# A decoder step with 32 experts: the last down rows in halves and narrowing blocks, the round count read earlier, the input scaled ahead of its squares' sum

## What is computed

```python
def _rmsnorm(x, g):
    xf = x.astype(jnp.float32)
    y = xf * lax.rsqrt(jnp.mean(xf * xf, axis=-1, keepdims=True) + NORM_EPS)
    return (y * g.astype(jnp.float32)).astype(x.dtype)
...
    def expert_block(args):
        xblk, e = args
        return (jax.nn.silu(xblk @ w_gate[e]) * (xblk @ w_up[e])) @ w_down[e]
...
    x = x + _hier_moe(_rmsnorm(x, norm_ffn_g), router_coarse, router_fine,
                      exp_w_gate, exp_w_up, exp_w_down)
```

## Time and profile before

| | |
|---|---|
| median of 3 runs | 1900.24 us (1899.46 to 1901.64) |
| the profiled execution | 1900.5 us |
| its span, first to last instruction | 1898.7 us |
| PE, DVE, ACT busy, share of the span | 82%, 33%, 14% |
| PEld busy | 47% |
| read from HBM, written | 499.87 MB, 9.82 MB |

### The profile page before, as it was taken

The page is one execution under the profiler, slowest core; times in us unless marked ns, Lnnn a source line. Parts: engine busy times, 40 slices in busy tenths (PEclk is TensorE's granted clock), DMA queues, the critical chain, the costliest instruction groups (busy, mean ns, idle before and its releaser), DMA issues.

```text
span 1898.7 us, 25843 instructions
## 1 busy us (share of the span) xinstructions
PE 1561.7 (82%) x8958; PEld 895.0 (47%) x8958; DVE 627.1 (33%) x1260; ACT 274.5 (14%) x592; POOL 62.2 (3%) x95
## 2 busy tenths in 40 slices
PE   8999999999999999999996674866758567576565
PEld 4676766666666666666763131321313223122121
DVE  6746565656464646520031010110101101020014
ACT  2222222222222222201012000000000000000002
POOL 1000000000000000000000000000000000000000
PEclk9999999999999999999998787877878778787878
DMA  7323232323232323267379999999999999999996
GB/s 286 111 92 109 87 107 84 114 82 119 82 119 82 119 82 119 75 223 285 133 321 426 428 427 428 429 428 429 427 429 427 429 429 427 430 427 430 427 407 241
DMA packets 71935, 510.61 MB, mean 269 GB/s; under 512 B 20496, under 2 KB 23696, under 8 KB 37808
## 3 DMA queue, kind: packets, MB, share of 16 engines
q1 hardware_dynamic: 71808, 509.60, 66.4%
q0 software_dynamic: 48, 0.12, 0.0%
HBM read 499.87 MB, written 9.82 MB: 268 GB/s over the span
## 4 chain that ended last, share of the span: by engine, by line
PE 53%; DMA 34%; DVE 7%; issue 3%; SPq 1%; DVEq 0%; ACT 0%; ACTq 0%
DMA arena<-w_up 22%; PE ps_PJ L720 20%; DMA arena<-w_down 12%; PE ps_C L1064 8%; DVE arena L1420 7%; PE ps_PJ L918 7%; SPq L559 1%; PE ps_C L1115 1%; PE ps_SB L1115 1%; PE ps_YB L1115 1%; PE ps_C L788 1%; PE ps_RT L1115 1%; PE ps_SB L757 1%; PE ps_C L797 1%; PE ps_RT L893 1%
## 5 line engine op out<-in xcount | busy, mean ns | idle before, releaser
L720 PE MATMUL ps_PJ<-arena 128*128 128x320 f32 x1792 | 540.7, 437 | 0.0
L1064 PE MATMUL ps_C<-arena 128*32 128x512 f32 x2048 | 284.2, 718 | 180.5 <-DMA arena<-w_gate 112.6
L720 PEld LDWEIGHTS ps_PJ<-arena 128*128 128x128 f32 x1792 | 323.7, 190 | 125.4 <-issue 23.9
L1420 DVE TENSOR_TENSOR arena<-arena,ps_PJ 128x512 f32<-128x512 f32 (+2 forms) x112 | 73.6, 657 | 612.6 <-PE ps_PJ L1018 493.4
L1064 PEld LDWEIGHTS ps_C<-arena 128*32 128x32 f32 x2048 | 79.0, 129 | 378.8 <-issue 376.4
L1420 DVE TENSOR_TENSOR arena<-arena 128x320 f32<-128x320 f32 (+11 forms) x310 | 161.4, 521 | 62.6 <-ACTq L421 25.7
L1147 ACT ACTIVATE arena<-ps_C 128x128 f32<-128x128 f32 (+3 forms) x68 | 27.4, 403 | 924.3 <-PE ps_C L1064 532.2
L918 PE MATMUL ps_PJ<-arena 128*128 128x320 f32 x512 | 142.5, 433 | 1.0 <-DVEq L421 1.0
L1147 ACT ACTIVATE arena<-arena 128x320 f32<-128x320 f32 (+11 forms) x206 | 97.9, 475 | 268.6 <-DVEq L421 88.2
L918 PEld LDWEIGHTS ps_PJ<-arena 128*128 128x128 f32 x512 | 95.7, 190 | 40.5 <-issue 4.0
L1115 PE MATMUL ps_C<-arena 128*32 128x512 f32 x224 | 41.5, 821 | 81.3 <-DMA arena<-w_down 80.4
(11 more groups left out here) (182 smaller groups left out, 1189.1 us busy)
## 6 DMA issues: line engine op xcount, KB each, us to landing
arena<-w_down SPq DMA_DIRECT2D x64, 2048.0 KB, 21.0
arena<-w_gate SPq DMA_DIRECT2D x61, 2048.0 KB, 21.1
arena<-w_up SPq DMA_DIRECT2D x61, 2048.0 KB, 20.1
arena<-win SPq DMA_DIRECT2D x59, 1024.0 KB, 4.8
arena<-w_out SPq DMA_DIRECT2D x16, 1024.0 KB, 7.7
arena<-w_gate SPq DMA_DIRECT2D x6, 1024.0 KB, 7.9
arena<-xT SPq DMA_DIRECT2D x8, 640.0 KB, 7.8
arena<-s_ret SPq DMA_DIRECT2D x8, 512.0 KB, 3.9
```

What stands on the lines that cost most here:

```text
L720: last = mm(pj(j)[:, 0:T], wt[j % NSLOT][:, kt, :], hT[:, kt, :], start=kt == 0, stop=kt == KT - 1)
L1064: last = mm((GB, UB)[u][h * CAP:(h + 1) * CAP, :], xg[:, kt, h * CAP:(h + 1) * CAP], w[h](k), start=kt == 0, stop=kt == KT - 1)
L1420: ins = build(*args)
```

## The change

**Down rows of the last quad.** Pieces 16 to 19 now hold the even row halves (rows 0 to 127 and 256 to 383) of one expert each, all 2048 columns. Pieces 20 and 21 hold the odd halves of two experts each, columns 0 to 1023. Piece 22 holds the odd halves of all four for columns 1024 to 1535. Piece 23 is two transfers of 1 MB: columns 1536 to 1791 (semaphore `early_in`) and 1792 to 2047. The column blocks are in the table `LAST`: three of 512 and two of 256. TensorE does the even rows of the first four blocks, then, for each block, the odd rows, the wait for the copy and `combine`; the even rows of the last block come just before its odd rows. ScalarE's copies and squares and VectorE's adds and gains follow the same table. An empty hand-over (`claim`, `nop`) keeps the two banks' count even.

**Rounds.** SyncE reads `nround` and branches ahead of its stores, which stand in both branches now; VectorE does so before the last quad of a round (`begin_round`, `end_round`). TensorE and ScalarE read it where they did.

**Start.** VectorE applies the gains to all parts before it adds the last two parts' squares. The semaphores `hT_in` and `x_in` become one set, `xT_in`.

```diff
+LAST = [(0, F), (F, F), (2 * F, F), (3 * F, F // 2), (3 * F + F // 2, F // 2)]
...
+            def odd_rows(h0, h1, a, b):
+                return w_down[h0:h1, :, a:b].rearrange("h (k e p) n -> e p h k n", k=2, e=2)[1, :, :, :, :]
...
+                    elif c < 5 * QUAD:
+                        src = w_down[NE - QUAD + c % QUAD, :, :].rearrange("(k e p) n -> p k n", k=2, e=2)[0, :, :, :]
...
+                    elif c < 5 * QUAD + 2:
+                        h0 = NE - QUAD + 2 * (c % QUAD)
+                        src = odd_rows(h0, h0 + 2, 0, 2 * F)
...
+                    elif c == 5 * QUAD + 2:
+                        src = odd_rows(NE - QUAD, NE, 2 * F, 3 * F)
...
-                        src = w_down[NE - QUAD:NE, :, n * F:(n + 1) * F].rearrange("h (k e p) n -> e p h k n", k=2, e=2)[e, :, :, :, :]
...
+                        for b, arrived in enumerate((sem("early_in"), ex_in[s])):
+                            src = odd_rows(NE - QUAD, NE, 3 * F + b * F // 2, 3 * F + (b + 1) * F // 2)
...
-            store_rows(0, out_y)
             sp.wait_ge(named["routed"], 1)
             r = sp.value_load(nround[0:1, 0:1], min_val=1, max_val=ROUNDS)
             with sp.If(r > 1):
+                store_rows(0, out_y)
...
             with sp.Else():
+                store_rows(0, out_y)
...
+                if last_quad:
+                    pe.wait_ge(named["gT_done"], it + 1)
+                    w4 = [piece_in(4 * QUAD + h, it).rearrange("p (k n) -> p k n", k=2) for h in range(QUAD)]
...
+                    for block in LAST[:-1]:
+                        last = even_rows(*block)
+                    last.then_inc(ex_used, QUAD)
+                    low = [piece_in(5 * QUAD + i, it).rearrange("p (h k n) -> p h k n", h=2, k=2) for i in range(2)]
+                    for i, (at, n_) in enumerate(LAST):
...
+                        elif i == 4:
+                            even_rows(at, n_)
+                            piece_in(5 * QUAD + 3, it)
+                            w = half_slot(1, it)
...
+                        last.then_inc(ex_used if i != 3 else sem("block_done"), 1)
+                        pe.wait_ge(named["yp_part"], len(LAST) * rd + i + 1)
+                        combine(at, n_)
...
-                if k0 >= 4:
-                    TT(squares[0], squares[0], squares_of(k0, 4).rearrange("p k n -> p (k n)"), ALU.add).then_inc(sq_used, 1)
+                if k0 == 4:
+                    TT(squares[0], squares[0], squares_of(4, 4).rearrange("p k n -> p (k n)"), ALU.add).then_inc(sq_used, 1)
+            for k0 in (8, 12):
+                TT(squares[0], squares[0], squares_of(k0, 4).rearrange("p k n -> p (k n)"), ALU.add)
```

More of the change, by code:

```diff
@@ L345, in build_program @@
         win_in = [sem(f"piece_in{s}") for s in range(NSLOT)]
-        const_in, hT_in, sq_done, sq_used = sem("const_in"), [sem(f"hT_in{i}") for i in range(4)], sem("sq_done"), sem("sq_used")
+        const_in, xT_in, sq_done, sq_used = sem("const_in"), [sem(f"xT_in{i}") for i in range(4)], sem("sq_done"), sem("sq_used")
         sum_done, hT_done = sem("sum_done"), sem("hT_done")
@@ L388, in build_program @@
         ex_in, ex_used = [sem(f"expert_in{s}") for s in range(NSLOT_C)], sem("expert_used")
-        x_in, x1T_done, tr_full, tr_free = [sem(f"x_in{i}") for i in range(4)], sem("x1T_done"), sem("transposed"), sem("x1_done")
+        x1T_done, tr_full, tr_free = sem("x1T_done"), sem("transposed"), sem("x1_done")
         r_in, gfin_in, out_y, out_more = sem("router_in"), sem("gfin_in"), sem("out_y"), sem("out_more")
@@ L1012, in gather, with combine @@
                 last.then_inc(x_full[b], 1)
-            def combine(n):
+            def combine(at, n_):
                 for t, (t0, nt) in enumerate(TT_):
                     b = claim()
-                    mm(XB[b][0:nt, :], gT[:, t0:t0 + nt], yp[:, n * F:(n + 1) * F], start=True, stop=True).then_inc(x_full[b], 1)
+                    mm(XB[b][0:nt, 0:n_], gT[:, t0:t0 + nt], yp[:, at:at + n_], start=True, stop=True).then_inc(x_full[b], 1)
             def piece_in(c, it):
@@ L1095, in experts @@
                     pe.wait_ge(named["d_free"], it)
[L1096 to L1110, removed]
+                for k in range(0 if last_quad else 2):
                     w = [piece_in(4 * QUAD + QUAD * k + h, it).rearrange("p (j n) -> p j n", j=2) for h in range(QUAD)]
@@ L1384, in round_of_experts @@
             def round_of_experts(rd, at_op):
-                half, at = EQ * XUSES // 2 * rd, EQ * rd
+                half, at = RUSES // 2 * rd, EQ * rd
                 n[0], n[1] = at_op, 0
@@ L1863, in experts @@
                 for q in range(2):
-                    for on, done_ in ((opening and q == 1, gathered), (before, combined), (more, gathered)):
-                        if on:
-                            done_(2 * q)
-                            done_(2 * q + 1)
+                    if opening and q == 1:
+                        gathered(2)
+                        gathered(3)
+                    if before:
+                        combined(2 * q * F, F)
+                        combined((2 * q + 1) * F, F)
+                    if more:
+                        gathered(2 * q)
+                        gathered(2 * q + 1)
                 dve.wait_ge(named["tanh_done"], it + 1)
```

115 lines of the change are left out of this document (76 added, 39 removed).

## The result

The changed kernel takes 1908.03 us, the median of 6 runs (1906.51 to 1909.58). The kernel before took 1900.46 us beside it (6 runs, 1898.56 to 1901.64). The ratio is 1.0039, 95% interval 1.0029 to 1.0049: **slower, by 7.6 us**, a small difference, but one clear of the noise. The forecast was 1904.1, range 1901.6 to 1907.0: the sign was right, the forecast loss was half of the measured one, and the time lies outside the range.

A forecast was written before the change was run, and what follows sets the result against it. The expert stage was taken as bound by its weight stream up to 1876.33, then by one serial chain. Close +4.8, clock +0.8, start -0.86, rounds -0.9 gave +3.8, called +4: 1904.1 us, range 1901.6 to 1907.0.

The forecast's parts named there:

- the sign: Whole kernel: slower than before, given a chance of 0.53, against 0.40 for same and 0.07 for faster.
- L1: Close: landing of pieces 20 and 21, which block 0's odd rows wait for, at 1862.9 (1862.6 to 1863.6).
- the stream: Down rows' transfers: 8 KB runs at 425 GB/s, 4 KB at 410; the stream ends about 2 us sooner.
- 7 to 14 KB: Kernel before, DMA: pieces with packets of this size read as running at 419 to 425 GB/s.
- The serial chain: Close: blocks 0 to 2 one after another at 5.78 us each, then 4.3 and 6.8; close +4.8 us.
- The clock: Block 0: may start at half clock after 3 to 5 us idle; cost 1.3, 0.6 of it charged, +0.8.
- The start: Kernel's start: PE's idle time for the last scaling goes and the gain goes through, -0.86 us.
- The rounds: Kernel's end: SyncE branches before its stores, so the end no longer waits for it, -0.9; VectorE's branch costs nothing.
- Half clock through the three blocks: Rival for the close, blocks 0 to 2: same serial close but at half clock, 1907.1 us, chance 0.09.
- The close that follows the last landing: Rival: blocks close as columns arrive, RECIPROCAL at 1880.2, 6.4 before; 1892 with start and end; chance 0.07.

The follow-up runs named there:

- e5_pipe: Changed kernel with TensorE combining each block one block later, behind the next block's odd rows: 1904.01 us, ratio to before 1.0017.
- e3_rows: Changed kernel with the start and rounds edits undone, so the down rows' edit alone: 1906.89 us, ratio to before 1.0043.
- e4_warm: Changed kernel with four unread 512-column matmuls between the even rows and the wait for pieces 20 and 21: 1904.43 us, ratio to before 1.0027.
- e6_byblock: Changed kernel with pieces 20 and 21 cut by column block in place of by pairs of experts: 1900.04 us, ratio to before 0.9999.
- e1_start: Kernel before with the start edit alone: 1899.6 us, ratio to before 1.0004.
- e8_narrow: Kernel before with rounds read ahead, start edit plus two empty instructions, and only the narrow last block of the down rows' edit: 1896.36 us, ratio 0.9978.
- e11_both: Changed kernel with the edits of e5_pipe and e6_byblock together: 1903.15 us, ratio to before 1.0014.
- e2_rounds: Kernel before with the round count read ahead on SyncE and VectorE alone: 1898.87 us, ratio to before 0.9995.
- e9_handover: Kernel before with the start edit, but both late sums of squares still signal their hand-over: 1899.15 us, ratio to before 0.9993.

## Why the prediction was half right

- **L1 and the stream.** Right: 32.64 us after the up rows against 32.4, 425 and 401 GB/s against 425 and 410, PE without work ahead of L1. One reading of mine was loose: "7 to 14 KB" is a mean that counts the few dozen small packets of the earlier trace rows; without them the packets are 8 and 16 KB. Nothing else hangs on it. That runs of 4 KB "are nearer to 8 KB in cost per byte" was my assumption: the 401 GB/s lie nearer to the 386 of 2 KB than to the 425 of 8 KB.
- **The serial chain.** Right: 6.08 and 5.78 against 5.78, 4.32 against 4.3, 7.02 against 6.8. e5_pipe shows that it is a chain: loosened, it runs in 4.80 to 5.01. The 0.3 us more in block 1 is PE's wait of 1.11 us for the copy in place of 0.82. I had called ScalarE tight, but that is not it, since ScalarE stood idle ahead of this copy:

```profile
1875.95 0.60 ACT L1190 ACTIVATE arena<-ps_SB 128x512 f32<-128x512 f32 x1 [0.57 <-PE ps_SB L1156]
```

  The kernel before has the same 1.11 us at the bank ps_SB (at 1859.78). Why this bank costs more is not shown; my 5.78 came from block 2 alone.
- **The clock: the term that failed.** I wrote that block 0 may start at half clock, that "the cost is 1.3 us as before", and added 0.6 of it, +0.8. That block 0 would run at half clock was right (0.50 from 1862.8 to 1872.8), the price was not. My own rows had such a case: behind 3.26 us of idle time the half took 3.19 us for 1.92, and I forecast 3 to 5 us of idle time. The chance of 0.6 was too low: all three traces with 3.7 us or more of idle time ahead of L1 have it (the changed kernel, e3_rows, e5_pipe). And 1.3 was the excess of one half only, of which the first 0.5 us still ran at full clock, and behind which the combination did too:

```profile
1880.33 3.11 PE L1018 MATMUL ps_PJ<-arena 128*128 128x512 f32 x6 [0.80 <-ACTq L421]
```

  Measured: 3.65 in the profiled run, 1.64 in e3_rows, 1.56 in e5_pipe (where the combination stands elsewhere), and nothing in e4_warm and e6_byblock, where the idle time is short or gone. By the ratios of e4_warm it is 2.3 us. So this price was high in the profiled run, and the term should have been about 2 us, with a range up to 3.7.
- **The start: the second step that failed.** "The gain goes through: -0.86". At 33 us it was there, larger than forecast (1.18). The loop took about 1 us of it back at a place that no row of the kernel before could show, and e1_start measures no gain (1.0004). The rest of the 1.02 us up to the up rows is the loop's branches, worse by 0.9 in this profiled execution than in before's, and this part is chance: in e4_warm, e5_pipe and e6_byblock, with the same code up to there, the up rows start at 1830.3 to 1830.5.
- **The rounds.** Right: 1.15 in the trace against 0.9. VectorE's branch cost nothing: its next instruction came 5.8 us after the branch, and VectorE still waited 44.95 us for PE behind it.
- **The rivals.** "Half clock through the three blocks" came near the time (1907.1) by luck and missed the place: blocks 1 and 2 ran at full clock. The close that follows the last landing did not come in the changed kernel; it is what e8_narrow gets by keeping blocks 0 to 2 in the order of their data.

Together: the medians lie 7.6 us apart where 3.9 was forecast. By the ratios the clock accounts for about 1.5 us of the difference (2.3 less 0.8) and the start for 0.9 to 1.7 (nothing or +0.8 in place of -0.86); the rest is within the intervals.

What stays open: why the clock stayed at half for 10.2 us in the changed kernel's trace, 6.8 in e3_rows and 3.4 in e5_pipe, with 4.37, 4.83 and 3.72 us of idle time; and what the two missing instructions do that costs the 0.14 us.

## What to carry to other kernels

When data come in order, cut the last transfers along the order in which the work can be finished; a piece that spans two results delays the first of them (here block 0 began 32.64 us after the last up rows in place of 28.67 in e6_byblock). Charge an idle gap ahead of a serial chain with the half clock of everything in the chain's first step, the combination too, or fill it (here block 0 took 9.43 us behind 4.37 us of idle time, 5.70 with the gap filled to 1.58). Loosening a chain pays only where its data are there: the edit that won 4.2 us in e5_pipe won nothing in e11_both. And one execution's mark can be off by more than the edit is worth (here 1 us of branches against a gain of 0.9): compare it over several traces before you explain it.

## What the runs showed of the hardware

- TensorE's granted clock fell to half while TensorE stood idle for its data (4.37 us in the changed kernel, 4.83 in e3_rows, 3.72 in e5_pipe), and came back 10.2, 6.8 and 3.4 us later. Behind 1.58 us of idle time (e4_warm) it did not fall. Ahead of the last half block it fell in e2_rounds (2.86 us of idle time) and not in e9_handover (2.89).
- VectorE's branch back in the pair loop cost 2.7 to 3.3 us, different from pass to pass and from execution to execution. Over the six in the chain of waits that is 17.0 to 18.8 us in the 13 traces, whose code in the loop is the same.
- Two instructions fewer ahead of a loop made one place in each pass 0.14 us slower (0.41 against 0.27 us of idle time), and two signals that nobody waits for undid it. What in the two instructions or their signals makes the 0.14 us, no run here shows.
- Packets of 8 KB ran at 425 GB/s and of 4 KB at 401 (changed kernel), where 2 KB had 386 (before).
